# An attention stage whose rotary turn leaves TensorE: six of eight query pairs are turned by transfers of 32-row blocks

## The reference

```python
def rope(x, pos):
    ...
    x1, x2 = xf[..., :half], xf[..., half:]          # half = 32 of 64
    return jnp.concatenate([x1 * cos - x2 * sin, x2 * cos + x1 * sin], axis=-1).astype(x.dtype)

q = (h @ w['w_q'][j]).reshape(bsz, t_len, ATT_HEADS, ATT_HEAD_DIM)
q = rope(rmsnorm(q, w['q_norm'][j]), pos)
out = window_attention(q, k_all, v_all, hist_valid, w['attn_sinks'][j]) @ w['w_o'][j]
```

## Time and profile before

| | us |
|---|---|
| median of 3 runs | 1199.32 (1198.93 to 1200.55) |
| profiled execution, its own time | 1199.57 |
| its span in the trace | 1197.8 |
| PE busy | 1186.2 (99%) |
| DVE, ACT, POOL busy | 873.5, 695.7, 247.3 |
| the attention stage, `scores(0)` to the last `weighted_sum` | from 899.8 to 952.7 in the span |

### The profile page before, as it was taken

The page is one execution under the profiler, slowest core; times in us unless marked ns, Lnnn a source line. Parts: engine busy times, 40 slices in busy tenths (PEclk is TensorE's granted clock), DMA queues, the critical chain, the costliest instruction groups (busy, mean ns, idle before and its releaser), DMA issues.

```text
span 1197.8 us, 26588 instructions
## 1 busy us (share of the span) xinstructions
PE 1186.2 (99%) x9797; PEld 1156.7 (97%) x9797; DVE 873.5 (73%) x1398; ACT 695.7 (58%) x1132; POOL 247.3 (21%) x351
## 2 busy tenths in 40 slices
PE   8999999999999999999999999999999999999998
PEld 8999999998989899999999999999998899999998
DVE  7767646999999868667745987787468767667448
ACT  6445435777686657555546765555368764444345
POOL 1000002423222102122344333232026410000001
PEclk9999999999999999999999999999999999999999
DMA  8765554755445365866786577656752256555552
GB/s 287 244 210 187 179 175 142 254 181 184 158 162 172 124 218 179 327 221 249 275 297 235 211 266 282 223 170 231 249 164 74 86 170 212 175 182 185 176 178 87
DMA packets 62144, 239.08 MB, mean 200 GB/s; under 512 B 7288, under 2 KB 8480, under 8 KB 57696
## 3 DMA queue, kind: packets, MB, share of 16 engines
q1 hardware_dynamic: 55728, 197.01, 48.6%
q0 software_dynamic: 6064, 40.66, 9.3%
q10 hardware_dynamic: 288, 0.54, 0.1%
HBM read 226.87 MB, written 13.39 MB: 201 GB/s over the span
## 4 chain that ended last, share of the span: by engine, by line
PE 88%; DVE 7%; ACT 3%; issue 1%; POOL 0%; DMA 0%; SPq 0%; DVEq 0%; ACTq 0%
PE bank L478 28%; PE bank L479 27%; PE bank L480 27%; DVE wlo L1519 2%; DVE xact L1787 1%; DVE xl L1538 1%; PE bank L842 1%; ACT under L1434 1%; PE bank L837 0%; ACT whi L1049 0%; DMA x<-xT 0%; PE bank L894 0%; PE bank L864 0%; DVE under L1566 0%; POOL gsq L2214 0%
## 5 line engine op out<-in xcount | busy, mean ns | idle before, releaser
L1519 DVE TENSOR_TENSOR wlo<-raw,whi 128x1024 fp32r<-128x1024 f32 x367 | 457.3, 1249 | 238.8 <-ACT whi L1049 237.3
L478 PE MATMUL bank<-xh,whi 128*128 128x264 f32 x2008 | 575.9, 287 | 3.5 <-DVE under L1566 1.5
L479 PE MATMUL bank<-xl,whi 128*128 128x264 f32 x2008 | 569.2, 283 | 0.0
L480 PE MATMUL bank<-xh,wlo 128*128 128x264 f32 x2008 | 568.8, 283 | 0.0
L1049 ACT ACTIVATE whi<-raw 128x1024 fp32r<-128x1024 f32 x367 | 385.4, 1054 | 242.6 <-PE bank L480 230.4
L478 PEld LDWEIGHTS bank<-xh,whi 128*128 128x128 f32 x2008 | 378.3, 188 | 7.9 <-issue 3.1
L479 PEld LDWEIGHTS bank<-xl,whi 128*128 128x128 f32 x2008 | 378.4, 188 | 0.8
L480 PEld LDWEIGHTS bank<-xh,wlo 128*128 128x128 f32 x2008 | 376.6, 188 | 0.0
L478 PE MATMUL bank<-hh,whi 128*128 (+1 forms) x896 | 255.5, 285 | 0.3 <-ACT gu L1402 0.3
L480 PE MATMUL bank<-hh,wlo 128*128 (+1 forms) x896 | 255.1, 285 | 0.0
L479 PE MATMUL bank<-hl,whi 128*128 (+1 forms) x896 | 254.4, 284 | 0.0
(11 more groups left out here) (331 smaller groups left out, 1024.0 us busy)
## 6 DMA issues: line engine op xcount, KB each, us to landing
raw<-weights SPq DMA_DIRECT2D x367, 512.0 KB, 3.5
under<-ssm POOLq DMA_DIRECT2D x8, 1024.0 KB, 7.2
xact<-ssm POOLq DMA_DIRECT2D x8, 1024.0 KB, 7.2
out_ssm_s<-xact POOLq DMA_DIRECT2D x8, 1024.0 KB, 6.0
xact<-dtx_rows POOLq DMA_DIRECT2D x5, 1024.0 KB, 10.1
zs<-dtx_rows POOLq DMA_DIRECT2D x2, 1024.0 KB, 13.6
x<-xT SPq DMA_DIRECT2D x4, 264.0 KB, 5.9
xact<-stat_rows POOLq DMA_DIRECT2D x2, 528.0 KB, 6.7
```

What stands on the lines that cost most here:

```text
L478: pe.matmul(out, whi[:, w, c], rh, start=start, stop=False)
L479: pe.matmul(out, whi[:, w, c], rl, start=False, stop=False)
L480: return pe.matmul(out, wlo[:, w, c], rh, start=False, stop=stop)
L1519: dve.tensor_tensor(wlo[:, s, :], raw[:, s, :], whi[:, s, :].bitcast(F32), ALU.subtract).then_inc(lo_ready, 1)
```

## The change

Pairs 0 and 1 are handled as before. For pairs 2 to 7 the rotation matmul is gone from `turn`; instead SP copies the query from `qf` into a buffer `q_swap`, four transfers of 32 rows x 264 each, with neighbouring 32-row blocks exchanged. DVE then multiplies `q_swap` by `sin_q`, a table with gain and sign in it that POOL makes once. DVE's `rope_sin` and `rope_add` of pair s-2 stand between `maxima` and the rest of slot s, where those of pair s-1 stood behind `probabilities`. SP's loop over the loads is cut open around the stage so that each group of transfers stands ahead of a certain load. On POOL the decode squares move from behind `query_cos(7)` to ahead of it.

```diff
+            def swap_query(t):
+                sp.wait_ge(a_free, A0["q"] + t + 1 + 4)
+                if t >= 4:
+                    sp.wait_ge(q_sin, t - 1)
+                for b in range(4):
+                    to, fr = 32 * b, 32 * (b ^ 1)
+                    sp.dma_start(q_swap[t % 2][to:to + 32, :], qf[fr:fr + 32, t, :]).then_inc(q_swapped[t % 2], 16)
+
+            load_rounds(2, Q_ROUNDS[0])
+            for u in range(Q_ROUNDS[0] * RING, Q_ROUNDS[1] * RING):
+                if u - 6 - U0["q"] in range(2, PAIRS):
+                    swap_query(u - 6 - U0["q"])
+                sp.wait_ge(lo_ready, u - RING + 1)
+                sp.dma_start(raw[:, u % RING, :], weights[u]).then_inc(raw_landed[u % RING], 16)
+            load_rounds(Q_ROUNDS[1], NU // RING)
...
             def turn(t):
                 pe.wait_ge(head_sq, t + 1)
-                pe.wait_ge(a_free, A0["q"] + t + 1 + 4)
+                if t < 2:
+                    pe.wait_ge(a_free, A0["q"] + t + 1 + 4)
...
                 for c in range(2):
-                    pe.matmul(bank[2][:, 264 + 2 * c:266 + 2 * c], sq3[:, t, 128 * c:128 * c + 128], blk[:, 0:P:64], start=True, stop=True)
-                pe.matmul(bank[2][:, 0:N], rot_q, qf[:, t, :], start=True, stop=True).then_inc(rot_done, 1)
+                    mm = pe.matmul(bank[2][:, 264 + 2 * c:266 + 2 * c], sq3[:, t, 128 * c:128 * c + 128], blk[:, 0:P:64], start=True, stop=True)
+                if t < 2:
+                    mm = pe.matmul(bank[2][:, 0:N], rot_q, qf[:, t, :], start=True, stop=True)
+                mm.then_inc(rot_done, 1)
...
                 if t >= 2:
                     dve.wait_ge(r_ready, t - 1)
+                    dve.wait_ge(q_swapped[t % 2], 64 * (t // 2))
...
-                dve.tensor_tensor(gu[:, 2 + t % 2, :], bank[2][:, 0:N], sinT, ALU.mult).then_inc(q_sin, 1)
+                if t < 2:
+                    dve.tensor_tensor(gu[:, 2 + t % 2, :], bank[2][:, 0:N], sinT, ALU.mult).then_inc(q_sin, 1)
+                else:
+                    dve.tensor_tensor(gu[:, 2 + t % 2, :], q_swap[t % 2], sin_q, ALU.mult).then_inc(q_sin, 1)
...
             for s_ in range(3, PAIRS):
                 maxima(s_ - 3)
-                if s_ == 3:
-                    rope_sin(1)
-                    rope_add(1)
+                rope_sin(s_ - 2)
+                rope_add(s_ - 2)
...
                 probabilities(s_ - 3)
-                rope_sin(s_ - 1)
-                rope_add(s_ - 1)
             maxima(5)
+            rope_sin(6)
+            rope_add(6)
             low_o(3)
...
+            pool.wait_ge(unit_used, U0["f1o1"] + FT + RING)
+            pool.tensor_scalar(sin_q, sinT, vs[:, V_QS:V_QS + 1], cs[:, C_SGN:C_SGN + 1], ALU.mult, ALU.mult)
```

More of the change, by code:

```diff
@@ L75 @@
 C_EPQ = C_WIN + 38
-NC_ = C_EPQ + 1
+C_SGN = C_EPQ + 1
+NC_ = C_SGN + 1
 G_F1, G_MIX, G_F2, G_PLE, G_KV = 0, 16, 32, 48, 64
 V_CW, V_CB, V_D, V_NG, V_ALOG, V_DTB, V_KN, V_QN, V_SINKD, V_SINK = 72, 200, 232, 248, 264, 265, 266, 267, 268, 269
-NV = 269 + AH
+V_QS = 269 + AH
+NV = V_QS + 1
 DT_STEPS = 15
@@ L139 @@
 PAIRS = 8
+Q_ROUNDS = [U0["q"] // RING, (U0["q"] + 6 + PAIRS) // RING + 1]
 QUERY_BANK = [0, 1, 3, 1, 0, 1, 0, 1]
@@ L190, in trunk_kernel @@
             spread_q = under[:, 30 * N:35 * N]
+            q_swap, sin_q = [under[:, (41 + b) * N:(42 + b) * N] for b in range(2)], under[:, 43 * N:44 * N]
             probs_t = [under[:, 8 * N + 1536 + 768 * b:8 * N + 2304 + 768 * b].rearrange("p (b n) -> p b n", b=2) for b in range(2)]
@@ L323, in trunk_kernel @@
         q_gains = sem("q_gains")
+        q_swapped = [sem("q_swapped0"), sem("q_swapped1")]
         mask_ready = sem("mask_ready")
@@ L449, in _, with load_rounds @@
                     sp.dma_start(vs[:, :], vec).then_inc(w_init, 16)
[L450 to L454, removed]
+            def load_rounds(first, last):
+                with sp.Fori(first, last) as i:
+                    for s in range(RING):
+                        sp.wait_ge(lo_ready, i * RING + (s - RING + 1))
+                        sp.dma_start(raw[:, s, :], weights[bass.ds(i * RING + s, 1)].rearrange("u p n -> p (u n)")).then_inc(raw_landed[s], 16)
+            def swap_query(t):
[12 more added lines that the diff above has]
+            load_rounds(Q_ROUNDS[1], NU // RING)
             for u in range(NU // RING * RING, NU):
@@ L2361, in _ @@
                 inverse_root(r4[:, 4 * t:4 * t + 4], m4[t % 2], u5[:, 0:4], 4, r_ready)
[L2362 to L2365, removed]
                 if t == 5:
@@ L2371, in _ @@
                     ins.then_inc(dec_sq, 1)
+                if t + 2 < PAIRS:
+                    query_cos(t + 2)
+                if t == 4:
+                    spread_queries(0)
             spread_queries(1)
@@ L2434, in constants @@
     c[:, C_EPQ] = 64 * EPS / D
+    c[:, C_SGN] = np.where(np.arange(P) % 64 < 32, -1.0, 1.0)
     c[:, C_WIN:C_WIN + 38] = np.arange(38)[None, :] == 18 + k // 64
@@ L2470 @@
     v += [np.broadcast_to(sinks[perm][None, :], (P, AH))]
+    v += [np.tile(a["q_norm"][0].reshape(2, 32)[::-1].reshape(64), 2)[:, None]]
     vec = np.concatenate(v, axis=1)
```

## The result

The changed kernel takes 1200.8 us (median of 22 runs, 1198.65 to 1204.25), the kernel before 1199.13 us (22 runs, 1198.3 to 1201.07). The ratio is 1.0015 with an interval of 1.0009 to 1.0021: 0.15% slower. The forecast was 1199.0 us, so the sign is wrong, though the time lies in the range.

The account below looks back on a forecast made before the run. PE, busy 99%, was taken as the bound, with ACT and DVE close behind; waits leave 0.3 us of at most 3.7. 1199.57 less 0.3 is 1199.3, less 0.25 for the median: 1199.0 us, range 1197.2 to 1201.5.

Parts of the forecast that it names:

- DVE's order eats what PE is spared: Likeliest case for the stage: most of PE's saving goes into waits, 0.3 us is left, 1199.0 us; chance 0.67.
- rivals 1 and 2: Faster cases: whole matmul price kept, 1195.6 us, chance 0.06; gain of slots 6 and 7 kept, 1197.9 us, 0.14.
- PE's later stages run one matmul after the other, and nothing there can give more back or add to it: Behind transposes(5): all engines keep their order, so the 0.3 us left there would reach the end unchanged.
- the wait at turn(7): Behind the loop: PE waits about 1 us for DVE's turn of pair 6; turn(7) can begin at 932.7, before 932.88.
- Scores(1) and scores(2): Early slots: they begin 0.25 and 0.1 us earlier, since PE then waits for ACT's mask.
- The price of the matmul: Slot 6 on PE: one rotation takes 0.62 us, so six give 3.7 us at most.
- Slot 5: DVE becomes last: PE waits 0.6 us for probabilities(2); transposes(2) begin at 919.15 instead of 919.18, nothing gained so far.
- Slots 6 and 7, and turn(7): PE last again: transposes(2) to scores(4) 4.80 us, scores(4) to scores(5) 5.64; scores(5) 1.3 earlier, turn(7) at 932.7.
- The ends of the range: Turn at 0.95 us each gives 0.5 less overall; at 1.15 to 1.2, 0.1 or 0.2 more; likeliest case 1198.3 to 1199.8.
- within 15%: In this stage PE, ACT and DVE were said to be busy within 15% of each other, read from slots 6 and 4.
- DVE's turn: On DVE behind the maxima: 1.0 us per turn taken, 0.95 further on, with 0.14 possible for two SBUF inputs.
- The transfers: SP's copies: issues of 0.33 us, no time cost, 0.2 to 1.8 us to spare for pair 7.

Follow-up runs that it names:

- e1: The changed kernel with the first two pieces of the embedding projection moved ahead of turn(7) on PE; 1200.64 us, ratio to before 1.0007.
- e2: The changed kernel with twelve idle matmuls added ahead of turn(7); 1199.80 us, ratio to before 1.0006.
- e5: The changed kernel with idle matmuls in three waits: 6 ahead of scores(2), 7 ahead of transposes(2), 12 ahead of turn(7); 1199.40 us, ratio to before 1.0002.
- e4: The kernel before with only DVE's turn moved behind the maxima, rotation matmuls kept and no transfers; 1202.30 us, ratio to before 1.0021.
- e6: The kernel before with DVE's turn moved behind the maxima and twelve idle matmuls ahead of turn(7); 1200.95 us, ratio to before 1.0011.
- e7: The changed kernel with DVE's low_p(1) in slot 4 instead of slot 5; 1199.15 us, ratio to before 1.0007.
- e8: The changed kernel with split_p(1) in slot 3, low_p(1) in slot 4, pair 7 by matmul, twelve idle matmuls ahead of turn(7); 1198.76 us, ratio to before 0.9994.
- e3: The changed kernel, transfers kept, with DVE's turn back behind the probabilities; 1201.69 us, ratio to before 1.0017.
- e9: The changed kernel with DVE's turn back behind the probabilities and pair 7 turned by the matmul; 1199.47 us, ratio to before 1.0003.
- e10: The changed kernel with split_p(1) in slot 3, low_p(1) in slot 4 and pair 7 by matmul, without idle matmuls; 1199.37 us, ratio to before 0.9998.

## Why the prediction was wrong

**The sum at full clock.** 1199.0 us was forecast and 1199.0 was measured over the six runs at the high clock; e1, e2 and e5 gave 1199.2 to 1199.65. So "DVE's order eats what PE is spared" is right, and rivals 1 and 2 are refuted: 1195.6 and 1197.9 us, where the changed kernel's fastest run of 22 took 1198.65. The agreement to the tenth is luck, though. Within the stage I forecast 0.3 us less to transposes(5); e1 and e5, whose clock did not fall there, have it at 38.00 and 38.12 us behind scores(0), 0.3 to 0.5 more than before's 37.66. The rest was made up outside the stage: PE was ahead before it began, by an amount that differs from execution to execution, and from the last weighted sum to the end the kernels with transfers take 0.2 us less (245.26 against 245.47), for a reason I have not looked into.

**The step that failed.** "PE's later stages run one matmul after the other, and nothing there can give more back or add to it", and ahead of it the wait at turn(7), which I foresaw ("about 1 us") and priced at its length alone. The wait was 1.51 us, and behind it came some 3 us at a granted clock of 0.50. From turn(7) to transposes(5) that is 5.68 us, against 4.62 before and 4.46 in e5, so 1.1 to 1.2 us. By the medians, the 16 of 22 runs with a lowered clock are 1.8 to 4.8 us longer, though only one of them was traced. The term for the clock was missing from the sum, from the rivals and from the bounds. e4 and e6 show it without the rest of the change, and e5, with all three waits filled, takes it away in 10 of 11 runs. The Trainium skill, "TensorE: Matmul & The Clock Gate", section "HAM oscillation — how this bites in real kernels", names idle gaps of PE as what brings the half clock. The traces agree in part: a fall came behind gaps of 1.51, 1.53 and 1.65 us, but not behind the one of 1.51 in e7 nor behind those of 1.5 near 231 us, and in e2 and e8 it came without a gap.

**Scores(1) and scores(2).** Forecast 0.25 and 0.1 us earlier against scores(0), with a wait for the mask: measured 0.16 and 0.0 (5.59 against 5.75, 12.22 against 12.21), waits of 0.34 and 0.83. Right in kind, and each 0.1 too good: the forecast gave 0.06 us from the mask's end to PE, for which it named no row, and in the changed kernel it is 0.14 and 0.15 (904.84 to 904.98, 911.46 to 911.61).

**The price of the matmul.** 0.62 us was forecast, with the weighted sum 0.36 behind the four sums; it is 0.43 behind them (922.83 to 923.26), and from transposes(2) to scores(4) are 4.86 us against 5.42 before. So a rotation was worth 0.56 us, and the most that six could give 3.4.

**Slot 5.** Right in kind, too small in size. Transposes(2) were to be 0.03 us earlier and are 0.48 later against scores(0) (19.82 against 19.34); PE waits 0.96 instead of 0.6. They begin where I put them (17.78 us behind scores(0), forecast 17.79). The term that was too small is their length, which I took over unchanged from before. DVE, after:

```profile
917.57 0.42 DVE L2095 TENSOR_TENSOR under<-under,small 128x256 f32<-128x256 f32 x1
917.92 1.23 DVE L2096 TENSOR_TENSOR under<-under,small 128x512 f32<-128x512 f32 x1
919.07 0.41 DVE L2081 TENSOR_REDUCE small<-bank 128x2 f32<-128x256 f32 x1
```

and POOL at the same time:

```profile
917.76 0.84 POOL L2363 TENSOR_TENSOR gu<-xact 128x264 f32<-128x264 f32 x1 [0.17 <-ACT xact L1451]
```

The same DVE instruction took 0.68 us in before:

```profile
917.97 0.68 DVE L2066 TENSOR_TENSOR under<-under,small 128x512 f32<-128x512 f32 x1
```

There POOL's product began at 918.69, when it was done. Against scores(0) two things moved towards each other. L2096 begins 0.40 us later (18.53 against 18.13). The product waits for ACT's copy of query 5 and begins 0.48 earlier (18.37 against 18.85), because ACT no longer waits for DVE's maxima; in before it did:

```profile
915.01 0.46 ACT L1434 ACTIVATE under<-bank,small 128x128 f32<-128x128 f32 x1 [0.38 <-DVE small L2055]
```

So the product falls on the probabilities, and L2096 takes 0.55 us more. In e7 the product begins at 918.14, just behind L2096 (917.44), which takes 0.68 again. The lock of "SBUF: two separate sides" (the Trainium skill, "SBUF — State Buffer") is what I had weighed for the new multiplication. The trace agrees, with 1.23 us against 0.68, but the instruction that it struck was another one.

**Slots 6 and 7, and turn(7).** The intervals nearly held: transposes(2) to scores(4) took 4.86 us (forecast 4.80), scores(4) to scores(5) 5.72 (5.64), scores(5) to turn(7) 3.24 (3.1). With the 0.5 us of slot 5 carried along, turn(7) stands 0.8 us later against scores(0) than forecast (33.64, forecast 32.86) and 0.6 later than before's 33.04. This part is no matter of the clock.

**The ends of the range.** By the forecast's own chain two turns at 0.95 would give 0.4 us less, not 0.5, and three at 1.15 to 1.2 would give 0.2 to 0.4 more, not 0.1 to 0.2. And the "within 15%" of three engines holds for slot 6 only; in slot 4 DVE was busy for 4.61 of 6.46 us. Neither bears on the outcome.

**DVE's turn.** 0.96 us with both inputs in SBUF (932.42 to 933.38), forecast 0.95 to 1.0. Right.

**The transfers.** They cost no time in the changed kernel: no wait of DVE names them. But I gave each issue 0.33 us from the rows of `out_y`, and they took nearly double. SP's issues of all 24, ns min/median/max:

```profile
L469 SPq DMA_DIRECT2D under<-xact x24: 507/590/601, 899.5 to 932.3; - x24
...
DMA to landing us min/median/max: 1.7/1.9/3.8
```

Four are 2.4 us and not 1.3 (2.72 for pair 7), so the last transfer had less to spare than I wrote. e3 and e9 show that the margin is real: a schedule in which the copy comes later pays 1.4 us. The 8 us that I had estimated from the Trainium skill, "DMA: Bandwidth & Descriptors", section "Anatomy of one DMA — SWDGE (gpsimd) path", for four transfers in a row did not come about. That section gives its 2.0 us of fixed cost for transfers issued from GpSimd, and these are SP's. They are issued 0.59 us apart, and the slowest landed 3.8 us after its issue and the median one 1.9, so they are under way together.

**The decode squares.** Worth nothing, as said: turn(7) waits for DVE.

## What to carry to other kernels

A wait of PE that grows from 0.3 to 1.5 us can cost more than the difference: in this stage the granted clock was half for some 3 us behind it in three of four traces, which cost 1.2 to 3.1 us. So in a tuned kernel whose PE is at 99% such a fall should be among the rivals of a forecast that adds a wait of 1 us or more, and the spread of the runs and their mean clock belong beside the median. Whether a fall follows depends on more than the wait's length, as the stage near 231 us shows. Where the wait can't be taken out, matmuls in it can hold the clock, even idle ones (e5, e6). And a piece taken from the engine that looks full (here six matmuls, 3.4 us) is worth only what the next ones in the ring can give: test that by moving a piece off those (e7), not by taking more from the first.

## What the runs showed of the hardware that I had not expected

- Granted clock 0.50 behind a gap of PE of 1.51 us (changed kernel), of 1.53 us (e4, where it stayed at 0.50 for 5.6 us) and of 1.65 us (e10), with a granted clock of 1.00 up to the gap and in it; and 1.00 throughout behind a gap of 1.51 us (e7) and of 1.5 us in another stage (all 14 traces).
- What lowers it in runs of kernels without long waits is open. In the profiled executions of e2 and e8, both at 0.998, it fell without such a gap and at the same piece of work, behind the last transposes. In e8 (window, the columns as above):

```profile
951.25:954.75 3.50, 3.50 (x23) 2.93 (x22) 2.54 (x6) 0.92 (x3) 0.00 (x0) 0.51 0.40 147
```

- SP takes 0.59 us for the issue of a transfer of 32 rows between SBUF and SBUF, against 0.33 for a load or a store of 128 rows; in e3 four of them took 3.73 us, for a reason not looked into.
- Whether shorter waits lower the clock too: with 1.0 to 1.14 us (e1, e3) 13 of 22 runs fell, as often as with 1.5, though no fall behind such a wait was traced. For 0.8 to 0.95 us it is open: e2 against e5 (4 and 1 runs of 11) is too few to tell, and e9 with waits of up to 0.83 us has 2 of 11.
- The sums of the odd pairs in columns of their own, so that turn(7) need not wait for DVE's turn of pair 6, were not tried: DVE's reading and PE's writing of one bank would no longer be in a fixed order.
